# Conditioning chunks of a two-block transformer kernel, read and multiplied one at a time or in pairs, on one Trainium2 core

## What is computed

```python
proj = rms_norm(x, g_mix) @ w_in            # first block: (256 x 2048) @ (2048 x 7536), float32
...
c_act = jax.nn.silu(c)                      # second block's condition: one row of 2048 numbers
mod = c_act @ w_ada + b_ada                 # (1 x 2048) @ (2048 x 12288), float32: 96 MB of weights
sh1, sc1, g1, sh2, sc2, g2 = jnp.split(mod, 6)
```

## Time and profile before

| | |
|---|---|
| median of three runs | 3203.69 us (3200.47 to 3208.19) |
| the profiled execution | 3206.84 us, of which its span 3205.0 us |
| TensorE busy | 3059.0 us, 95% of the span |
| granted TensorE clock, mean over the span | 0.978 |
| the first stream | about 30 us to 445 us of the span |

### The profile page before, as it was taken

The page is one execution under the profiler, slowest core; times in us unless marked ns, Lnnn a source line. Parts: engine busy times, 40 slices in busy tenths (PEclk is TensorE's granted clock), DMA queues, the critical chain, the costliest instruction groups (busy, mean ns, idle before and its releaser), DMA issues. The chain is left out here.

```text
span 3205.0 us, 43840 instructions
## 1 busy us (share of the span) xinstructions
PE 3059.0 (95%) x17864; PEld 2445.3 (76%) x17864; DVE 2066.4 (64%) x2332; ACT 1512.3 (47%) x1822; POOL 20.0 (1%) x10
## 2 busy tenths in 40 slices
PE   7999978998899999999899989999998999999997
PEld 7888855966787776766688878877786788888886
DVE  5557547365868778785548858755666666555565
ACT  4345432143656566574444465555445444444443
POOL 0000001000000000000000000000000000000000
PEclk9999978999999999999999999999999999999998
DMA  7989868087979888794476654575666555555552
GB/s 267 335 266 341 283 214 346 4 302 272 340 274 320 282 285 319 262 341 143 148 232 215 215 187 152 190 250 168 239 225 221 192 190 186 194 184 194 185 190 72
DMA packets 358321, 739.09 MB, mean 231 GB/s; under 512 B 19977, under 2 KB 118422, under 8 KB 344583
## 3 DMA queue, kind: packets, MB, share of 16 engines
q1 hardware_dynamic: 342916, 711.64, 65.0%
q10 hardware_dynamic: 15236, 25.06, 2.1%
HBM read 710.00 MB, written 26.65 MB: 230 GB/s over the span
## 5 line engine op out<-in xcount | busy, mean ns | idle before, releaser
L286 DVE TENSOR_TENSOR moe_w_lo<-ring,moe_w_hi 128x1024 fp32r<-128x1024 f32 x384 | 461.5, 1221 | 158.0 <-ACT moe_w_hi L276 150.5
L276 ACT CAST moe_w_hi<-ring 128x1024 fp32r<-128x1024 f32 x384 | 402.3, 1049 | 271.9 <-PE psum L302 268.8
L286 DVE TENSOR_TENSOR mx_w_lo<-ring,mx_w_hi 128x1024 fp32r<-128x1024 f32 (+1 forms) x288 | 346.8, 1210 | 281.5 <-ACT mx_w_hi L276 277.8
L276 ACT CAST mx_w_hi<-ring 128x1024 fp32r<-128x1024 f32 (+1 forms) x288 | 296.5, 1036 | 423.9 <-PE psum L302 407.8
L286 DVE TENSOR_TENSOR mlp_w_lo<-ring,mlp_w_hi 128x1024 fp32r<-128x1024 f32 x256 | 313.6, 1226 | 282.9 <-ACT mlp_w_hi L276 282.0
L276 ACT CAST mlp_w_hi<-ring 128x1024 fp32r<-128x1024 f32 x256 | 268.0, 1048 | 408.3 <-PE psum L302 408.3
L302 PE MATMUL psum<-mx_w_hi,mx_a_hi 128*128 128x496 f32 (+1 forms) x1024 | 406.8, 397 | 6.0 <-DVE mx_w_lo L286 4.0
L302 PE MATMUL psum<-mx_w_lo,mx_a_hi 128*128 128x496 f32 (+1 forms) x1024 | 398.7, 389 | 0.0
L302 PE MATMUL psum<-mx_w_hi,mx_a_lo 128*128 128x496 f32 (+1 forms) x1024 | 398.5, 389 | 0.0
L286 DVE TENSOR_TENSOR in_w_lo<-ring,in_w_hi 128x628 fp32r<-128x628 f32 x192 | 155.3, 813 | 185.1 <-ACT in_w_hi L276 183.6
L302 PE MATMUL psum<-in_w_hi,in_a_hi 128*128 128x314 f32 x768 | 243.8, 317 | 2.4 <-DVE in_a_lo L249 1.3
(11 more groups left out here) (604 smaller groups left out, 5574.0 us busy)
## 6 DMA issues: line engine op xcount, KB each, us to landing
ring<-in_w_ada SPq DMA_DIRECT2D x72, 1024.0 KB, 9.0
ring<-in_w_e_gate SPq DMA_DIRECT2D x64, 1024.0 KB, 5.5
ring<-in_w_e_up SPq DMA_DIRECT2D x64, 1024.0 KB, 6.6
ring<-in_w_e_down SPq DMA_DIRECT2D x64, 1024.0 KB, 5.6
ring<-in_w_up SPq DMA_DIRECT2D x64, 1024.0 KB, 5.2
ring<-in_w_down SPq DMA_DIRECT2D x64, 1024.0 KB, 5.1
ring<-in_w_in SPq DMA_DIRECT2D x64, 992.0 KB, 5.2
ring<-in_w_in SPq DMA_DIRECT2D x96, 628.0 KB, 5.4
```

Of the source, the lines that this page charges most:

```text
L276: self.nc.scalar.copy(self.w[0][:, self._half(j, half), :, 0:cols], self.view[:, slot, ks, 0:cols]).then_inc(self.hi_done, 1)
L286: self.nc.vector.tensor_tensor(self.w[1][:, q, :, 0:cols], self.view[:, j % self.slots, ks, 0:cols], self.w[0][:, q, :, 0:cols].bitcast(F3 ...
```

## The change

The places of the conditioning chunks are moved so that chunk 2i takes the place of chunk 2i+1: 12, 12, 20, 20, 27, 27, 35, 35, ... The last place (tick 185) stays. TensorE signals that buffers are free only after the second of a pair, with one count for both, and the waits are rewritten to that count. SP therefore issues the two loads of a pair one after the other. What is computed, and by which instructions, stays the same.

```diff
     def spare_tick(self, j):
-        return 9 + 15 * j // 4
+        return 9 + 15 * (j | 1) // 4

     def spare_sync(self, sp):
         for j in range(self.SPARE):
             yield max(0, self.spare_tick(j - 2) + 1)
             if j >= 2:
-                sp.wait_ge(self.spent, j - 1)
+                sp.wait_ge(self.spent, j // 2)
             sp.dma_start(self.tiles[j % 2], self.source(0, j)).then_inc(self.filled[j % 2], 16)
...
-            mm.then_inc(self.spent, 1)
+            if j % 2:
+                mm.then_inc(self.spent, 1)

     def spare_scalar(self, sc):
         for part in range(self.SPARE // KT):
             yield self.spare_tick(part * KT + KT - 1) + 1
-            sc.wait_ge(self.spent, part * KT + KT)
+            sc.wait_ge(self.spent, (part * KT + KT) // 2)
             self.row_out(sc)
...
-                sp.wait_ge(ada.spent, ada.SPARE)
+                sp.wait_ge(ada.spent, ada.SPARE // 2)
```

## The result

| | before | after |
|---|---|---|
| median of 12 runs each | 3204.30 us (3200.17 to 3209.41) | 3210.67 us (3204.25 to 3216.84) |
| ratio after / before, 95% interval | | 1.0016 [1.0009, 1.0023] |
| the profiled execution | 3206.84 us | 3206.07 us |
| last matmul of the first stream starts at | 445.30 us | 449.03 us |
| the sum of TensorE's waits in the stream | 3.9 us | 12.0 us |

What follows compares the result with a forecast made beforehand. TensorE, busy 95% of the span, was taken to set the stream's pace. Terms -7.7 + 0.5 + 0.6 + 0.3 = -6.3 us took the median 3203.69 to a forecast of 3197.4 us, 0.2% less; range 3193 to 3203.

Steps and rivals of the forecast that it cites:

- Changes of shape, -7.7: On TensorE, a pair of chunks takes 2.04 us against 2.36 for two single ones; 24 pairs save 7.7 us.
- no saving: Rival, chance 0.05: a pair on TensorE costs two single chunks (spanning 2.65 us), only losses remain, about 3204 us.
- Places behind a score product, +0.5: On TensorE, chunks behind a score product cost 0.18 us less; seven such places become four, losing 0.5 us.
- signals, nothing: One signal less per pair and the same number of waits, in queues that run ahead; costed at nothing.
- The second load of a pair: On SP's queue, it lands 2.7 us behind the first, at 9.2 us, in time by 0.7 us; nothing charged at most places.
- The 0.6 us charged at tick 42: Where SP waits for a store and reads back, the second load comes late by 0 to 1.3 us; middle taken.
- the one on loads: Step on DMA loads: no load moves forward, so never more asked than before; nothing charged except 0.6 us at tick 42.
- TensorE's waits for `in_w_lo`: Sign named beforehand: such waits behind pairs would show the step on loads to be wrong.
- The attention step, +0.3: At 152.24 us TensorE, waiting for DVE's step behind a late cast, waits some 0.3 us more than the 0.87 before.
- the other waits are paced by TensorE itself and stay: Claim that TensorE's stream waits other than the one at the attention step do not change; nothing charged.
- late in part: Rival, chance 0.18: late conditioning loads at six places, or late stream loads delaying ACT, cost 2 to 6 us; 3199.5 to 3203.5.
- Slower: Rival, chance 0.05: second loads land after 12.9 us, TensorE waits 3.0 us at each of six places; some 3215 us.

Runs made afterwards that it cites:

- e4: The changed kernel without 46 of its 48 conditioning loads, the two loaded buffers being reused; stream's last matmul at 438.19 us, ratio to before 0.9985.
- e3: The kernel before, single chunks, without 46 of its 48 conditioning loads; stream's last matmul at 444.52 us, ratio to before 1.0009.
- e8: The changed kernel, unedited, measured and profiled a second time; stream's last matmul at 448.64 us, ratio to before 1.0004.
- e1: The changed kernel with a third buffer and conditioning loads issued one at a time at the ticks of before; stream's last matmul at 439.87 us, ratio 0.9989.
- e5: The changed kernel with the second load of each pair issued two ticks later; stream's last matmul at 451.32 us, ratio to before 1.0019.
- e6: The changed kernel with the attention's read-backs taken from an input and SP's waits for stores left out; stream's last matmul at 446.87 us, ratio 1.0002.
- e12: The changed kernel with a third buffer, loads spread only for six pairs near small tables or read-backs; stream's last matmul at 441.85 us, ratio 0.9995.
- e13: The changed kernel with a third buffer, loads spread except for six pairs near small tables or read-backs; stream's last matmul at 443.43 us, ratio 0.9990.
- e11: Repeat of e1: the changed kernel with a third buffer and loads one at a time; stream's last matmul at 439.92 us, ratio 0.9986.
- e9: The changed kernel with two more buffers up to chunk 39 and both loads of a pair four ticks earlier; stream's last matmul at 449.86 us, ratio 1.0008.
- e10: The changed kernel with two more buffers up to chunk 39 and both loads of a pair two ticks earlier; stream's last matmul at 441.92 us, ratio 0.9998.

## Why the prediction was wrong

- *Changes of shape, -7.7:* right. The pair spans 2.33 us, 2.04 net, to the rounding, and e4 against e3 gives -6.3 of the -7.2 that this term and the next add up to. The rival "no saving" is excluded, and so is its pair of 2.65 us.
- *Places behind a score product, +0.5, and signals, nothing:* not contradicted; no experiment took them apart.
- *The second load of a pair:* right for itself. The working gave a margin of 0.7 us at the tight places; there it was 1.9 in the change (tick 27, the working's own place), and the smallest of all was 0.95 us (tick 50; 0.36 in e8). The working had compared the second load with the time at which the first is used, 0.9 us too early. No wait of L569 is in the profile after. The 0.6 us charged at tick 42 did not come, because SP went on sooner: it began the read-back at 108.42, not at 110.95, and issued the pair at 111.29 and 111.84, ahead of the 113.65 of before.
- *The step that failed* is the one on loads, in the words "at no moment has more been asked of the DMA engines than before" and "I charge nothing at most places". It asked only when the conditioning loads land. It said nothing of the stream loads behind them, of which ACT already waited for 28. The one at 112.46 found two megabytes ahead of it and landed after 11.8 us. The Trainium skill's section "Queues, rings and completion order" ("DMA: Bandwidth & Descriptors") states that each engine takes its descriptors in ring order; the prediction drew from it that the stream loads can't pass a pair, and then priced only the second load of the pair. The trace agrees with the ring order at the stream load, 11.8 us against 8.6. Spreading the loads gave 9.2 us back (e1), of which the forecast had 0.6. TensorE's waits for `in_w_lo` (3.9 us in 5, before 1.2 in 1) are the sign that the prediction itself had named for this step being wrong.
- *The attention step, +0.3:* right place and right mechanism, sized too small: the wait went from 0.87 to 2.59, +1.7 (1.81 in e8), and to 0.9 again in e1; and the lower clock behind it cost another 1.6 us, for which there was no term. L3120 (2.4 us) and L3074 for `ring` (1.3) were not foreseen: "the other waits are paced by TensorE itself and stay" was wrong, since DVE's and ACT's steps stand behind late casts in the same queues, and TensorE, ahead of its old pace, meets one of them even in e4.
- *The rivals:* "late in part" named this mechanism in its last clause, but priced it at 2 to 6 us, and it cost about 10: 11.0 lost, less 1.0 of the pairs themselves. "Slower" came out in its sign, not by its mechanism. Waits of L569 of its kind come in e5, six of them with 10.1 us, but only three (at ticks 27, 117 and 147) come next behind a tick that it named (20, 110 and 140), and there they follow from a load moved two ticks on.
- *What the working left out* is the carry from one delay to the next. e6 puts 2.2 us on the part that runs through the stores; what more there is of it e12 and e13 leave open. Each place looked at alone had room; nothing asked how soon the room came back after it was used, in a stream in which the DMA engines have a mean share of 0.85.

What stays open is the exact interplay: that the late loads cost the time is shown by e1, e11 and e13, and where e9 loses against e10 is shown at three places, but why a burst at one tick is cheap and dear two ticks on is not reduced to a rule, and whether bursts make each other dearer is not shown.

## What to carry to other kernels

When a change makes an engine free its buffers in groups, the transfers come in groups too; then look at the loads that stand behind the group in the same queue, and at the engine that already waits for these, before the group's own. If the saving is on the engine that computes, keep the loads at their old pace with one more buffer: here that turned +3.7 us of the stream into -5.4. Beside full DMA engines a margin counted place by place is not enough, because a delay is carried on by in-order queues, and by stores whose landing the next loads wait for. And a wait of TensorE can cost more than its length: of the five longest looked at here (2.3 to 4.0 us) four had the lower clock behind them.

## What the runs showed of the hardware

- A stream load of 628 KB lands after 8.6 us behind one megabyte and a read-back, after 11.8 behind two and the same read-back, and after 12.0 behind two with small tables ahead (one load each). The difference of 3.2 us is near the 2.7 us that a megabyte takes at the highest rate seen.
- In the stretch from 120 to 130 the DMA engines are as full after as before (1.05 and 1.04) but move 357 instead of 373 GB/s, while ACT waits for them.
- Behind waits of TensorE of 2.59 (the change), 2.27 (e6), 2.36 (e9) and 4.0 us (e5) the granted clock fell to its lower level for a stretch, which cost 1.6 us in the change against e8; behind 2.70 (e13) and 1.81 us (e8) it stayed full.
- The time behind the first stream scatters by 12 us between profiled executions (2753 to 2765), also for one kernel (e1 2765.4, e11 2754.9), while the stream's end repeats within 0.4. It was shortest where the mean granted clock of the execution was highest (2753.3 us at 0.981, e13) and longest where it was lowest (2762.3 and 2765.4 us at 0.977, e3 and e1). For an edit within one stage that stage's end is the sharper measure.
